# Moving banks, waits and copies in a four-stage transformer kernel: down projection, even and odd attention

## The chip, the core and the metric

The kernel runs on one core of a Trainium2 chip. A core has a matrix engine (TensorE, PE in the rows; its weight loads are PEld), a vector engine (VectorE, DVE), a scalar engine (ScalarE, ACT), GpSimd (POOL) and SyncE (SP), which issues transfers. Each follows its own list of instructions in order, and they wait for each other on semaphores. TensorE writes its results into eight PSUM banks of 128 x 512 f32. The metric is the device time of one execution in microseconds; lower is better.

## The reference, cut to what matters

512 tokens of width 1024 pass through two blocks. All tensors are f32.

```python
# first block: attention and convolution (left out here), then the FFN
x = x + conv_ffn(rms_norm(x, norm2_g), ffn_w_up, ffn_dw_w, ffn_dw_b, ffn_w_down)
#   conv_ffn: u = causal_dwconv(h @ w_up, dw_w) + dw_b;  a, v = split(u)
#             return (silu(a) * v) @ w_down              # 2816 -> 1024
x = rms_norm(x, final_g)
# second block, layer 0 ("even"): 8 dense heads (A) and 8 latent heads (B), 512 keys each
sc = q @ k.T * scale;  p = softmax(sc);  o = p @ v       # per block of 128 queries
x = x + gate * (concat(oa, ob) @ w_out)
# layer 1 ("odd"): 16 heads, |query - key| <= 128, alibi bias and a sink
sc = q @ k.T * scale - slope * |rel|                     # 3 neighbouring blocks of keys
m = max(max(sc), sink);  p = exp(sc - m)
o = (p / (sum(p) + exp(sink - m))) @ v
x = x + gate * ((o * silu(g)) @ odd_w_out)
return rms_norm(x, final_norm)
```

## The kernel before, in words

Activations are kept transposed: a chunk is 128 features by 512 tokens. Weights come in 171 units of 128 x 1024 f32. SP loads a unit into one of five slots once the unit five places before it is done (`unit_done`), and GpSimd splits it into a high and a low part (`whi`, `wlo`, lines 1040 to 1044; `w_split`). A product of a unit with the activations is made of threes of matmuls, high x high, high x low and low x high, since one alone would lose precision. Helper `unit` (line 446) makes such a product in one bank, eight threes, 24 matmuls, all recorded at line 461.

Every list of instructions is written out by hand. A bank is handed out by `bank.take(pe, pool, key)` (line 156): a pool is a tuple of bank numbers that is used in turn, with a counter that belongs to the tuple's value, and taking a bank makes TensorE wait for whoever frees its last content.

**Down stage.** The FFN's second product has 22 units (`FC`), each with all eight output chunks, so it accumulates in all eight banks at once: `down_block(i, n)` (line 754) is the three matmuls (line 760) of unit i into bank n. Unit i needs its weights and chunk i of the FFN's hidden values, `("fa", i)`. Units 0 to 17 are done one after the other, with the chunks in the order 2, 3, 6, 7, 4, 5, 1, 0; the last four (`LATE` on) chunk by chunk, so that chunk 0 is ready first and VectorE can add it to the residual (line 2085). Banks 4 and 5 hold, during the up stage before it, a copy of a vector from which VectorE makes the modulation (`ada_unit`, line 2010, `modp`); the other six are the up stage's own and are freed one by one by the depthwise convolution's last operations (lines 2026 to 2044).

**Even attention.** 32 steps (`ab_steps`), four query blocks for each of 8 pairs of heads. In step i TensorE makes the scores of step i (banks 1 and 2; line 844 or 849), the transposes of step i-2 (banks 4 and 5; line 857) and the values of step i-3 (line 870 on), with a rowsum spread every fourth step and parts of weight units as filler in the first ten. VectorE takes the scores' maximum (line 2188), ScalarE then makes the exponentials of step i (`ab_exp`, line 1445) and copies the transposed block of step i-2 out of banks 4 and 5 (`ab_copy`, line 1453), in this order.

**Even output projection.** Eight units `("eout", i)`. The first three use banks 0, 1 and 2 and are begun between the last attention steps; their last threes stand together at line 937. The other five take the pool `WIDE`, (0, 1, 2, 3). VectorE adds each result to the residual (`residual`, line 2254), which frees its bank. Behind them come the first odd units: `raw_units` takes banks 0, 1, 2 in turn, and bank 3 for the small bias products (line 478).

**Odd attention.** 32 steps again (`c_steps`), four query blocks qt for each of 8 pairs. A step has scores against two or three key blocks (256 or 384 columns; line 959), three to eight threes of an `("og", p + 1)` unit as filler (none in every fourth step, none in the last four), the transposes of step i-2 (line 969), the values of step i-3 (`c_values`, line 987), and every fourth step a spread (line 999). The values of a pair are sums over the four key blocks kt, all in the one bank 6; key block 0 was added in the second step of the pair, 1 in the third, 2 and 3 in the fourth. Bank 6 is freed by VectorE's `c_out` of the pair before (lines 2317 and 2324), which stands behind the gate of line 2164 and ahead of the next maximum (line 2290). ScalarE has exponentials (line 1518) and then the copy of one half (line 1527); VectorE copies the other half (line 2302).

## Time and profile before

| | us |
|---|---|
| median of 3 runs (1366.27 to 1368.05) | 1367.89 |
| the profiled execution | 1367.87 |
| its span, from the first instruction to the last | 1365.3 |
| TensorE busy in it | 1316.9 |
| VectorE busy | 820.5 |
| GpSimd busy | 637.6 |
| ScalarE busy | 440.2 |
| mean granted TensorE clock | 0.987 |

The profiled execution is as long as the median; 2.6 us of it lie outside the span. TensorE is busy for 96% of the span, so what it waits for, and the stretches in which its clock is low, are read one by one: the views used are the page, the waits of TensorE, the timeline and the windows.

### The profile page before, as it was taken

The page shows a single profiled execution, that of the slowest core. Times are in us where ns is not written, and L with a number is a line of the kernel's source. Part 1 is how long each engine was busy: PE and PEld are TensorE (multiplying, and loading weights), DVE is VectorE, ACT ScalarE, POOL GpSimd, SP SyncE. Part 2 cuts the span into 40 slices and gives each one's busy share as a digit, 9 for nine tenths or more (in the row PEclk, how much of TensorE's full clock was granted, in tenths as well). Part 3 has the DMA queues.
Part 4 walks back from the last instruction along what each step waited for, and adds up shares of the span by engine and source line. Part 5 has one row for each costly group of instructions (what it writes and reads, how often), then busy time and mean ns, then how long its engine had stood idle before and what let it go on. Part 6 is the DMA issues. An engine that isn't in the chain of part 4 may idle for free. (4 is left out here: it accounts for less than half of the span.)

```text
span 1365.3 us, 19690 instructions
## 1 busy us (share of the span) xinstructions
PE 1316.9 (96%) x7254; PEld 1036.5 (76%) x7254; DVE 820.5 (60%) x1586; ACT 440.2 (32%) x948; POOL 637.6 (47%) x523
## 2 busy tenths in 40 slices
PE   7999999999999999999999999999999999999996
PEld 5897766688888888888788788876556788767675
DVE  4898689914554777777572456535655254156643
ACT  4201455523122112222110332255656122244521
POOL 5865222246676666666576365532000365622230
PEclk9999999999999999999999989999999999999998
DMA  5622110112343455555543124211000123211111
GB/s 177 239 68 77 32 41 24 46 62 83 103 169 123 169 187 200 199 186 191 178 155 95 44 93 152 88 47 32 0 1 1 62 83 93 93 38 41 32 47 62
DMA packets 37522, 130.24 MB, mean 95 GB/s; under 512 B 4544, under 2 KB 4800, under 8 KB 37184
## 3 DMA queue, kind: packets, MB, share of 16 engines
q1 hardware_dynamic: 26640, 93.11, 21.3%
q10 hardware_dynamic: 10800, 35.98, 7.1%
q8 instruction: 58, 0.95, 0.3%
q14 instruction: 24, 0.20, 0.0%
HBM read 126.98 MB, written 2.10 MB: 95 GB/s over the span
## 5 line engine op out<-in xcount | busy, mean ns | idle before, releaser
L1044 POOL TENSOR_TENSOR wlo<-raw,whi 128x1024 fp32r<-128x1024 f32 x171 | 417.0, 2438 | 14.3
L1040 POOL TENSOR_TENSOR whi<-raw,ones 128x2 fp32r<-128x2 f32 x171 | 40.9, 239 | 677.5 <-DMA raw<-in_w 677.5
L461 PE MATMUL bank<-ysplit,whi 128*128 128x512 f32 x984 | 314.5, 398 | 2.1 <-DVE xbuf L2254 2.1
L461 PE MATMUL bank<-hhi,whi 128*128 128x512 f32 x536 | 218.1, 407 | 0.4 <-DVE arena L2164 0.4
L461 PEld LDWEIGHTS bank<-ysplit,whi 128*128 128x128 f32 x984 | 184.4, 190 | 38.9 <-issue 3.2
L461 PE MATMUL bank<-hhi,wlo 128*128 128x512 f32 x536 | 209.9, 392 | 0.0
L461 PE MATMUL bank<-hlo,whi 128*128 128x512 f32 x536 | 209.4, 391 | 0.0
L461 PE MATMUL bank<-ysplit,wlo 128*128 128x512 f32 x496 | 194.9, 393 | 0.0
L1041 POOL TENSOR_SCALAR whi<-raw 128x1022 fp32r<-128x1022 f32 x171 | 185.8, 1086 | 0.0
L461 PEld LDWEIGHTS bank<-hhi,whi 128*128 128x128 f32 x536 | 100.9, 188 | 25.6 <-issue 6.6
L461 PEld LDWEIGHTS bank<-hhi,wlo 128*128 128x128 f32 x536 | 100.9, 188 | 22.0
L461 PEld LDWEIGHTS bank<-hlo,whi 128*128 128x128 f32 x536 | 101.2, 189 | 18.1
L461 PEld LDWEIGHTS bank<-ysplit,wlo 128*128 128x128 f32 x496 | 94.0, 189 | 20.1
L1706 DVE SCALAR_TENSOR_TENSOR arena<-first,arena 128x512 f32<-128x512 f32 x120 | 105.6, 930 | 0.2
L1331 ACT ACTIVATE arena<-bank,cols 128x512 f32<-128x512 f32 x44 | 34.3, 779 | 177.7 <-DVE bank L2026 177.7
L760 PE MATMUL bank<-hhi,whi 128*128 128x512 f32 x176 | 70.0, 398 | 5.6 <-DVE modp L2010 3.3
L2188 DVE CUSTOM_DVE_ANT_0 arena<-bank,arena 128x512 f32<-128x512 f32 x64 | 44.2, 690 | 47.2 <-PE bank L849 28.9
L1445 ACT ACTIVATE arena<-arena,nmax,stat 128x512 f32<-128x512 f32 x64 | 51.6, 807 | 60.8 <-DVE nmax L2195 31.4
L760 PE MATMUL bank<-hlo,whi 128*128 128x512 f32 x176 | 69.7, 396 | 0.0
L760 PE MATMUL bank<-hhi,wlo 128*128 128x512 f32 x176 | 69.5, 395 | 0.0
L2026 DVE TENSOR_TENSOR bank<-bank,arena 128x512 f32<-128x512 f32 x44 | 30.7, 698 | 50.4 <-PE bank L461 50.4
L2010 DVE CUSTOM_DVE_ANT_0 arena<-bank,arena 128x512 f32<-128x512 f32 x80 | 51.7, 683 | 0.0
(315 smaller groups left out, 2100.5 us busy)
## 6 DMA issues: line engine op xcount, KB each, us to landing
raw<-in_w SPq DMA_DIRECT2D x171, 512.0 KB, 3.6
arena<-in_ada ACTq DMA_DIRECT2D x48, 512.0 KB, 4.3
xbuf<-in_xT ACTq DMA_DIRECT2D x12, 256.0 KB, 5.6
xbuf<-in_w ACTq DMA_DIRECT2D x1, 2048.0 KB, 8.9
first<-in_w ACTq DMA_DIRECT2D x1, 2048.0 KB, 8.4
out_t<-xbuf SPq DMA_DIRECT2D x8, 256.0 KB, 2.2
xbuf<-in_xT SPq DMA_DIRECT2D x4, 256.0 KB, 6.4
first<-in_uq ACTq DMA_DIRECT2D x1, 768.0 KB, 6.5
```

Source lines behind the costliest of these rows:

```text
L461: m = mm(b[:, :], w[:, s, k * P:(k + 1) * P], x, start=(k == 0 and part == 0), stop=(k == DC - 1 and part == 2))
L760: m = mm(b[:, :], w[:, u % WS, n * P:(n + 1) * P], x, start=(i == 0 and part == 0), stop=(i == FC - 1 and part == 2))
L1040: g.tensor_tensor(whi[:, s, 0:2], raw[:, s, 0:2], ones[:, :], ALU.mult)
L1041: g.tensor_scalar(whi[:, s, 2:D], raw[:, s, 2:D], 1.0, 1.0, ALU.mult, ALU.mult)\
L1044: g.tensor_tensor(wlo[:, s, :], raw[:, s, :], whi[:, s, :].bitcast(F32), ALU.subtract)\
L1331: A(ua[:, i % 4, :], bank.of(("up", i))[:, :], ACT.Identity, scale=col("ffw", order_up(i) * 3 + 2), bias=col("ffb", order_up(i)))\
L1445: A(abp[:, s % 3, half, :], abp[:, s % 3, half, :], ACT.Exp, bias=nmax[:, x:x + 1], scale=ab_scale(p, half, qt), accum_out=rsum[:, x:x + 1 ...
L1706: V.scalar_tensor_tensor(cacc[:, c, :], z[:, c, k:k + T], w, cacc[:, c, :], ALU.mult, ALU.add)\
L2010: V.tensor_tensor_reduce(ada[:, j % 2, at], bank.tiles[CACT[half]][:, :], ada[:, j % 2, at], 1.0, 0.0, ALU.mult, ALU.add, acc[:, j // (3 * ...
L2026: V.tensor_tensor(b[:, :], b[:, :], spread2, ALU.mult).then_inc(*dve_did.up(("un", i)))
L2188: link(V.tensor_tensor_reduce(abp[:, s % 3, half, :], bank.of(("S", "AB", s, half))[:, :], zero, 1.0, -3.0e38, ALU.add, ALU.max, nmax[:, x ...
```

## The change

There are five edits.

1. Down stage, start: units 0 and 1 are done together, in two parts. First chunks 2, 3 and 7 of both, then 6, 4, 5, 1 and 0 of both. The wait for `modp` stands at bank 4, no longer ahead of the stage. The later units have the order 2, 3, 7, 6, 4, 5, 1, 0.
2. Down stage, end: units 18 to 20 first add their chunks 0 and 1, each when its weights are there; then unit 21 is waited for, and its chunks 0 and 1 are added; the other chunks are as before.
3. Even output projection: units 3 to 7 take the pool (3, 0, 1, 2) in place of (0, 1, 2, 3). That tuple is the value of `E_BANKS` (line 115), too.
4. Odd attention: the values of a pair are all made in its fourth step.
5. Both attentions, ScalarE: the copy of step i-2 stands ahead of the exponentials of step i. VectorE's list is as it was.

```diff
--- before.py
+++ after.py
@@ -178,7 +178,7 @@
 H_BANKS = (6, 7)
 UP, CACT = (0, 1, 2, 3, 6, 7), (4, 5)
 N_FILL, N_S, N_O = (0,), (1, 2), (3, 6)
-EOUT_BANKS = (0, 1, 2)
+EOUT_BANKS, EOUT_REST = (0, 1, 2), (3, 0, 1, 2)
 AB_FILL_BANK, AB_S, AB_O = (0,), (1, 2), (3, 6)
 C_FILL, C_S, C_T, C_O, C_R = (0, 3), (1, 2), (4, 5), (6,), (7,)
 
@@ -762,17 +762,27 @@
                 return m
 
             LATE = FC - 4
-            pe.wait_ge(*dve_did.at(("ada", ADA_UP - 1)))
-            for i in range(FC):
-                u = UNIT[("down", i)]
-                pe.wait_ge(w_split.sem, u + 1)
+
+            def down_rows(i):
+                pe.wait_ge(w_split.sem, UNIT[("down", i)] + 1)
                 pe.wait_ge(*dve_did.at(("fa", i)))
-                for n in (2, 3, 6, 7, 4, 5, 1, 0) if i < LATE else ():
-                    if i == 0:
-                        bank.take(pe, (n,), ("down", n))
+
+            for part in (2, 3, 7), (6, 4, 5, 1, 0):
+                for i in range(2):
+                    down_rows(i)
+                    for n in part:
+                        if n == 4 and i == 0:
+                            pe.wait_ge(*dve_did.at(("ada", ADA_UP - 1)))
+                        if i == 0:
+                            bank.take(pe, (n,), ("down", n))
+                        m = down_block(i, n)
+                    if n == 0:
+                        m.then_inc(*unit_done.up(UNIT[("down", i)]))
+            for i in range(2, LATE):
+                down_rows(i)
+                for n in (2, 3, 7, 6, 4, 5, 1, 0):
                     m = down_block(i, n)
-                if i < LATE:
-                    m.then_inc(*unit_done.up(u))
+                m.then_inc(*unit_done.up(UNIT[("down", i)]))
 
             def double_sums(part):
 
@@ -784,8 +794,13 @@
                 if part:
                     m.then_inc(*pe_did.up(("fe", "sum")))
 
+            for i in range(LATE, FC - 1):
+                down_rows(i)
+                for n in range(2):
+                    down_block(i, n)
+            down_rows(FC - 1)
             for n in range(DC):
-                for i in range(LATE, FC):
+                for i in range(LATE if n >= 2 else FC - 1, FC):
                     m = down_block(i, n)
                     if n == DC - 1:
                         m.then_inc(*unit_done.up(UNIT[("down", i)]))
@@ -936,7 +951,7 @@
             for j in range(len(eout)):
                 eout[j](DC - 1)
             for i in range(len(eout), DC):
-                unit("eout", i, src=e_parts)
+                unit("eout", i, src=e_parts, pool=EOUT_REST)
             raw_units("o", 1, RAW_O, raw_o, lambda part: sums_once("o", part), lambda: spread("o", 0))
             for i in range(len(RAW_O), DC):
                 unit("oq", i, first=(lambda k: dve_did.at(("o", "h", k))) if i == len(RAW_O) else None,
@@ -971,15 +986,14 @@
                     m.then_inc(*pt_done.up(("C", i, half)))
 
             def c_values(i):
+
                 p, qt = c_steps[i]
-                if qt == 0:
+                if qt < TT - 1:
                     return
                 pe.wait_ge(*ptc.at(("C", i)))
                 pe.wait_ge(*ptd.at(("C", i)))
-                if qt == 1:
-                    bank.take(pe, C_O, ("O", "C", p))
-                b = bank.tiles[C_O[0]]
-                for kt in (qt - 1,) if qt < TT - 1 else (qt - 1, qt):
+                b = bank.take(pe, C_O, ("O", "C", p))
+                for kt in range(TT):
                     q0 = max(kt - 1, 0)
                     nq = min(kt + 1, TT - 1) - q0 + 1
                     for half in range(2):
@@ -987,8 +1001,7 @@
                         m = mm(b[64 * half:64 * half + 64, q0 * P:(q0 + nq) * P], ov[:, kt, g * HD:(g + 1) * HD],
                                pt_c(p, half, kt, q0 - kt + 1, nq), start=(kt == 0), stop=(kt == TT - 1),
                                skip_group_check=True)
-                if qt == TT - 1:
-                    m.then_inc(*pv_done.up(("C", p)))
+                m.then_inc(*pv_done.up(("C", p)))
 
             def c_spread(p):
                 pe.wait_ge(*dve_did.at(("C", "rinv", p)))
@@ -1464,10 +1477,10 @@
                 if i in PREP_V:
                     tt = i - PREP_V[0]
                     prep_copy("vB", tt, vB[:, tt, :], P)
+                if 2 <= i < n + 2:
+                    ab_copy(i - 2)
                 if i < n:
                     ab_exp(i)
-                if 2 <= i < n + 2:
-                    ab_copy(i - 2)
                 if i in PREP_K:
                     h = PREP_K[i]
                     prep_copy("KF", h, KF[h % 4][0:64, :], 64)
@@ -1531,10 +1544,10 @@
             n = len(c_steps)
             og_evac(0)
             for i in range(n + 5):
+                if 2 <= i < n + 2:
+                    c_copy(i - 2)
                 if i < n:
                     c_exp(i)
-                if 2 <= i < n + 2:
-                    c_copy(i - 2)
                 if i >= 4 and i % TT == 0 and i <= n:
                     p = i // TT - 1
                     act.wait_ge(*dve_did.at(("C", "sink", p)))
```

How TensorE's list changes is shown at three places. The first is the start of the down stage (line 760). Before, the twelve first matmuls:

```order
L760 MATMUL bank2<-hhi,whi 128x512 [waits dve_did,w_split]
L760 MATMUL bank2<-hlo,whi 128x512
L760 MATMUL bank2<-hhi,wlo 128x512
L760 MATMUL bank3<-hhi,whi 128x512 [waits dve_did]
L760 MATMUL bank3<-hlo,whi 128x512
L760 MATMUL bank3<-hhi,wlo 128x512
L760 MATMUL bank6<-hhi,whi 128x512 [waits dve_did]
L760 MATMUL bank6<-hlo,whi 128x512
L760 MATMUL bank6<-hhi,wlo 128x512
L760 MATMUL bank7<-hhi,whi 128x512 [waits dve_did]
L760 MATMUL bank7<-hlo,whi 128x512
L760 MATMUL bank7<-hhi,wlo 128x512
```

In the changed kernel, the first of each three where a bank or a wait is new:

```order
L760 MATMUL bank2<-hhi,whi 128x512 [waits dve_did,w_split]
L760 MATMUL bank2<-hlo,whi 128x512
L760 MATMUL bank2<-hhi,wlo 128x512
L760 MATMUL bank3<-hhi,whi 128x512 [waits dve_did]
...
L760 MATMUL bank7<-hhi,whi 128x512 [waits dve_did]
...
L760 MATMUL bank2<-hhi,whi 128x512 [waits dve_did,w_split]
...
L760 MATMUL bank6<-hhi,whi 128x512 [waits dve_did,w_split]
...
L760 MATMUL bank4<-hhi,whi 128x512 [waits act_did,dve_did]
```

Bank 6 is moved behind bank 7 and behind a second round over banks 2, 3 and 7, and bank 4 is the first to name what line 2010 writes. Before, a wait for that stood ahead of the first row.

The second place is the even output projection: the first matmul of each of its units 3 to 7 and, last, of the first odd unit (line 461) and its bias product (line 478). Before:

```order
L461 MATMUL bank2<-ysplit,whi 128x512 [waits dve_did,w_split]
...
L461 MATMUL bank3<-ysplit,whi 128x512 [waits dve_did,w_split]
...
L461 MATMUL bank0<-ysplit,whi 128x512 [waits dve_did,w_split]
...
L461 MATMUL bank1<-ysplit,whi 128x512 [waits dve_did,w_split]
...
L461 MATMUL bank2<-ysplit,whi 128x512 [waits dve_did,w_split]
...
L461 MATMUL bank0<-ysplit,whi 128x512 [waits dve_did,w_split]
...
L478 MATMUL bank3<-shr,whi 128x2 [waits dve_did]
```

In the changed kernel:

```order
L461 MATMUL bank0<-ysplit,whi 128x512 [waits dve_did,w_split]
...
L461 MATMUL bank1<-ysplit,whi 128x512 [waits dve_did,w_split]
...
L461 MATMUL bank2<-ysplit,whi 128x512 [waits dve_did,w_split]
...
L461 MATMUL bank3<-ysplit,whi 128x512 [waits dve_did,w_split]
...
L461 MATMUL bank0<-ysplit,whi 128x512 [waits dve_did,w_split]
...
L461 MATMUL bank0<-ysplit,whi 128x512 [waits dve_did,w_split]
...
L478 MATMUL bank3<-shr,whi 128x2 [waits dve_did]
```

Unit 3 has bank 0 in place of bank 2; unit 7 had bank 2 and now has bank 0, which the first odd unit takes next.

The third place is the odd attention, within one pair: transposes, values and scores in the third step, and values and scores in the fourth. Before (lines 969, 987, 959):

```order
L969 MATMUL bank4<-ident,arena 128x128 [waits ptc,p_ready]
L969 MATMUL bank4<-ident,arena 128x128
L969 MATMUL bank5<-ident,arena 128x128 [waits ptd,p_ready]
L969 MATMUL bank5<-ident,arena 128x128
L987 MATMUL bank6<-arena 64x384 [waits ptd,ptc]
L987 MATMUL bank6<-arena 64x384
L959 MATMUL bank1<-split_r,ysplit 128x384 [waits sm_ready]
...
L987 MATMUL bank6<-arena 64x384 [waits ptd,ptc]
L987 MATMUL bank6<-arena 64x384
L987 MATMUL bank6<-arena 64x256 x2
L959 MATMUL bank1<-split_r,ysplit 128x256 [waits sm_ready]
```

In the changed kernel the same three lines are 984, 1001 and 974:

```order
L984 MATMUL bank4<-ident,arena 128x128 [waits ptc,p_ready]
L984 MATMUL bank4<-ident,arena 128x128
L984 MATMUL bank5<-ident,arena 128x128 [waits ptd,p_ready]
L984 MATMUL bank5<-ident,arena 128x128
L974 MATMUL bank1<-split_r,ysplit 128x384 [waits sm_ready]
...
L984 MATMUL bank4<-ident,arena 128x128 [waits ptc,p_ready]
L984 MATMUL bank4<-ident,arena 128x128
L1001 MATMUL bank6<-arena 64x256 [waits dve_did,ptd,ptc]
L1001 MATMUL bank6<-arena 64x256
L1001 MATMUL bank6<-arena 64x384 x4
L1001 MATMUL bank6<-arena 64x256 x2
L974 MATMUL bank1<-split_r,ysplit 128x256 [waits sm_ready]
```

The third step has no values now, and the fourth has those of all four key blocks, with the wait for bank 6 (`dve_did`).

## Rows read from the trace of the kernel before

**Rows 1.** Page: busy us and share by engine, and TensorE clock by fortieth
```profile
PE 1316.9 (96%) x7254; PEld 1036.5 (76%) x7254; DVE 820.5 (60%) x1586; ACT 440.2 (32%) x948; POOL 637.6 (47%) x523
...
PEclk9999999999999999999999989999999999999998
```

**Rows 2.** Waits of TensorE, whole span: engine, place <- releaser: us, times, longest
```profile
PE bank L857 <- ACT arena L1453: 5.5, 7, 2.2
...
PE bank L760 <- DVE modp L2010: 3.3, 1, 3.3
...
PE bank L987 <- DVE arena L2324: 2.1, 2, 1.6
```

**Rows 3.** Timeline at the start of the down stage: start, us, engine, line, operation
```profile
660.03 0.69 DVE L2010 CUSTOM_DVE_ANT_0 arena<-bank,arena 128x512 f32<-128x512 f32 x1
...
660.77 0.79 PE L760 MATMUL bank<-hhi,whi 128*128 128x512 f32 x1 [3.33 <-DVE modp L2010]
...
662.81 0.69 DVE L2044 TENSOR_TENSOR arena<-bank,arena 128x512 f32<-128x512 f32 x1
...
664.10 0.40 PE L760 MATMUL bank<-hhi,wlo 128*128 128x512 f32 x1
...
675.67 0.39 PE L760 MATMUL bank<-hhi,wlo 128*128 128x512 f32 x1
```

**Rows 4.** Timeline at the last four units of the down stage, TensorE
```profile
762.64 0.66 PE L760 MATMUL bank<-hhi,whi 128*128 128x512 f32 x1 [2.26 <-POOL wlo L1044]
...
766.36 0.39 PE L760 MATMUL bank<-hhi,whi 128*128 128x512 f32 x1
```

**Rows 5.** Timeline of the even output projection and of what follows it
```profile
1076.29 1.44 DVE L2254 SCALAR_TENSOR_TENSOR xbuf<-bank,modc,xbuf 128x512 f32<-128x512 f32 x2 [8.38 <-PE bank L461]
...
1078.84 0.74 DVE L2254 SCALAR_TENSOR_TENSOR xbuf<-bank,modc,xbuf 128x512 f32<-128x512 f32 x1
...
1079.73 0.79 PE L461 MATMUL bank<-ysplit,whi 128*128 128x512 f32 x2 [2.10 <-DVE xbuf L2254]
...
1109.03 0.40 PE L461 MATMUL bank<-ysplit,whi 128*128 128x512 f32 x1
...
1109.23 0.75 DVE L2254 SCALAR_TENSOR_TENSOR xbuf<-bank,modc,xbuf 128x512 f32<-128x512 f32 x1 [2.50 <-PE bank L461]
```

**Rows 6.** Windows: a stretch; busy us of each engine; TensorE clock; DMA
```profile
1080.20:1083.70 3.50, 3.50 (x10) 2.68 (x10) 0.64 (x2) 0.66 (x2) 3.42 (x3) 0.51 0.51 199
```

**Rows 7.** Timeline at the end of the even attention
```profile
1050.25 1.04 PE L857 MATMUL bank<-ident,arena 128*128 128x128 f32 x8
...
1052.18 0.81 ACT L1445 ACTIVATE arena<-arena,nmax,stat 128x512 f32<-128x512 f32 x1 [2.54 <-DVE nmax L2195]
...
1053.79 1.05 ACT L1453 ACTIVATE arena<-bank 128x512 f32<-128x512 f32 x2
...
1054.51 1.11 PE L857 MATMUL bank<-ident,arena 128*128 128x128 f32 x8 [2.20 <-ACT arena L1453]
```

**Rows 8.** Timeline of the odd attention, an inner step and the end
```profile
1233.98 0.48 DVE L2290 CUSTOM_DVE_ANT_0 arena<-bank,arena 128x256 f32<-128x256 f32 x1
...
1234.27 0.65 PE L987 MATMUL bank<-arena 128*64 128x256 f32 x4
...
1234.85 0.79 PE L959 MATMUL bank<-split_r,ysplit 64*128 64x384 f32 x6
...
1292.38 0.65 PE L987 MATMUL bank<-arena 128*64 128x256 f32 x4 [1.59 <-DVE arena L2324]
...
1292.56 0.48 DVE L2290 CUSTOM_DVE_ANT_0 arena<-bank,arena 128x256 f32<-128x256 f32 x1
...
1293.19 0.80 PE L959 MATMUL bank<-split_r,ysplit 64*128 64x384 f32 x6 [0.15 <-DVE nmax L2290]
...
1303.56 1.97 PE L987 MATMUL bank<-arena 128*64 128x384 f32 x12
...
1305.33 1.07 PE L999 MATMUL bank<-ident,rinv 128*64 128x128 f32 x16
```

## The prediction

> **What bounds the kernel now.** I read the page first: TensorE is busy for 1316.9 of 1365.3 us [rows 1], so the time is its list of instructions, plus its waits, plus what a low clock adds. The clock line has one tenth less in three places of forty, so low stretches are short and have to be looked for in the timeline. Then I read the waits of TensorE: 5.5 us for ScalarE's copies in the even attention, 3.3 us for `modp` ahead of the down stage, 2.1 us for bank 6 in the odd attention [rows 2]. The timeline shows two more, 2.26 us for weights before the last four down units [rows 4] and 2.10 us for a bank in the even output projection [rows 5]. The edits aim at just these five. For each I ask whether the wait goes, and what is late next.
>
> **Clock.** Three of the waits are followed by matmuls at half rate. At full rate 51 matmuls of the down stage take 675.67 - 664.10 = 11.57 us, 0.227 each; after the first wait, the 8 intervals from 660.77 to 664.10 take 3.33 us in place of 1.82, so 1.5 us are lost [rows 3]. After the second, the 9 intervals from 762.64 to 766.36 take 3.72 us in place of 2.04, 1.7 lost [rows 4]. After the third the granted clock is 0.51, 1.2 GHz, for 3.5 us [rows 6], again 1.7 us lost. The 2.20 us wait at 1054.51 and the 1.59 us one at 1292.38 are followed by transposes and values in which I see no such stretch [rows 7, 8]. A wait that goes takes its low stretch with it.
>
> **Start of the down stage.** The first matmul can start at the end of the up stage, 3.33 us before 660.77 [rows 3], so near 657.4, if banks 2, 3 and 7 are free; they belonged to convolutions finished earlier, since those of the last two up units hold banks 0 and 1. Part one is 18 matmuls, 4.1 us, until 661.5. Bank 6 is the first of part two; bank 4, three matmuls on, is wanted at 662.2, when the last read of it, at 660.03 for 0.69 us, is done [rows 3]. Bank 0 is last, behind another 9 matmuls, at about 664.2; VectorE's last operation on it starts at 662.81 and takes 0.69 us, until 663.5 [rows 3]. All waits are covered, the tightest by 0.7 us. Gain 3.3 + 1.5 = 4.8 us. The slots of units 0 and 1 come free later within their pair, but unit 1 is done after 48 matmuls, 10.9 us, as ever.
>
> **Last four units.** TensorE waits 2.26 us for unit 21 [rows 4]. Units 18 to 20 now bring 3 x 2 x 3 = 18 matmuls, 4.1 us, ahead of it: the wait is covered with 1.8 us to spare. Chunk 0 is finished 21 matmuls after the start in place of 12, 2.0 us later, but chunk 1 after 24 as before, and VectorE's first step with chunk 0 is one addition alone. Gain 2.3 + 1.7 = 4.0 us.
>
> **Copies first, even attention.** At the end, the transposes at 1050.25 could be copied 0.72 us later (1053.79 to 1054.51 is what lies between a copy's start and the transposes that it frees a bank for, and I take the same the other way), at 1051.0. But exponentials that begin at 1052.18 stand ahead, so the copy starts at 1053.79 and TensorE waits 2.20 us [rows 7]. Copies first, it finds its bank at about 1051.7. Exponentials begin no sooner than the maximum allows, 1052.18, by which time a copy of 1.05 us from 1051.0 is done [rows 7]: nothing is delayed. All seven waits, 5.5 us [rows 2], have this form. TensorE then reaches the next scores sooner and could wait for VectorE's maximum; I take that at 0, at worst half is given back. Gain 5.5 us, bounds 2.7 and 5.5.
>
> **Even output projection.** Unit 3 now takes bank 0, which VectorE frees with the first of the two operations of 1.44 us from 1076.29, at 1077.0 [rows 5]. TensorE wants it 2.10 us before 1079.73, at 1077.6. The wait goes, and the low stretch: 2.1 + 1.7 = 3.8 us. But the counter of the tuple (3, 0, 1, 2) has run on through nine E units and stands at its second entry, so unit 7 gets bank 0 again, and the first odd unit, which takes bank 0, waits for the addition of unit 7. That addition starts at 1109.23; it takes 0.75 us, and from the end of such an addition to TensorE's start is 0.15 (1078.84 + 0.74 to 1079.73) [rows 5]. The unit starts at 1110.1 in place of 1109.03: a new wait of 1.1 us. Net gain 2.7 us (1.0 if this wait too were followed by a low stretch).
>
> **Values in the fourth step, odd attention.** The number of matmuls is the same. A short block of values has a start of its own: 4 records of 256 columns from 1234.27 to 1234.85 take 0.58 us, 12 with four times the columns from 1303.56 to 1305.33 take 1.77, 0.44 for a quarter [rows 8]; 0.14 us for each of 16 blocks that go is 2.2 us at most. But where bank 6 was waited for, VectorE is what is late: it has the gate, `c_out` and then the maxima in a row, and TensorE's next scores need the second of these. From the second maximum at 1292.56 to the scores at 1293.19 is 0.63 us. So these scores stay at 1293.19, whether or not values stand ahead of them: the 1.59 us wait for bank 6 [rows 8] becomes one of 2.4 us for the maxima. Within the pairs the same rule caps the gain: the second maximum at 1233.98 allows scores at 1234.6, 0.24 us sooner than 1234.85 [rows 8], and not the 0.58 of the block. The other 0.34 us are lost again in the fourth step, and what remains of merging is about 0.05 a pair, 0.4 in all. At the end the last pair loses: its 12-record block could begin beside the last copies, now all 16 records, 1.77 x 1.25 = 2.2 us, wait for them. I put 0.44 us for the extra quarter and 0.66 for the copy (0.55 us and its signals, an estimate by the lengths above), 1.1 us. Net: a loss of 0.7 us; bounds from a gain of 2.1 + 2.2 = 4.3 to a loss of 2.5 (0.7 and a low stretch of 1.7 after the new wait of 2.4). ScalarE's order in this stage changes little: TensorE waited for its copies only in the last steps.
>
> **Sum.** 4.8 + 4.0 + 5.5 + 2.7 - 0.7 = 16.3 us. The profiled execution took 1367.87 us, within 0.02 of the median, so the time follows as 1367.87 - 16.3 = 1351.6 us.
>
> **A rule on the clock.** All three waits that I credit with a low stretch have one in the trace [rows 3, 4, 6], and others do not [rows 7, 8]. The Trainium skill, "TensorE: Matmul & The Clock Gate", section "What's actually happening", says that the activity monitor runs freely and does not start with the kernel, so that where the clock turns differs from run to run. By that rule only a part of the 4.9 us is there in the average execution; by the rows it is all there. Its result is rival 1.
>
> **Rivals.**
> 1. The low stretches are chance: the median before holds about half of them, and as many appear elsewhere after. For it: waits of 2.26 and 2.10 us had one, one of 2.20 had none. Against: the profiled run has all three and is no slower than the median. Gain 16.3 - 2.4 = 13.9, or, with one more after the 2.4 us wait, 12: 1354 to 1356 us.
> 2. Values in one block pay: VectorE is not what is late, both waits for bank 6 go and the block starts are saved. Against it stand the maxima at 1292.56. 16.3 + 0.7 + 4.3 = 21.3: 1346.6 us.
> 3. Copies first only move the wait in the even attention to the scores' banks. Gain 16.3 - 2.7: 1354.3 us.
> 4. The other side: the fourth step, 1 us longer by its values, pushes the scores that follow it, so VectorE enters each pair's chain of gate, `c_out` and maxima late and the 2.4 us wait that I expect once appears in all eight pairs, 19 us. It decides if the fourth step's delay exceeds what filler covers. 1367.9 - 17.0 + 19.2 = 1370.1 us. Against: seven of the pairs have eight threes of filler, and only there does VectorE have 0.2 us and more to spare.
> 5. A bank that is not free in the down stage makes edit 1 do nothing: 16.3 - 4.8 gives 1356.4 us.
>
> **Numbers.** My forecast 0.55, rival 1 0.17, rival 2 0.08, rival 3 0.12, rival 4 0.03, rival 5 0.05. The range is 1347.5 to 1356: it holds the forecast, rivals 1 and 3, and part of 2, and the bounds of the even attention and of the new wait. What a measurement can tell from no change is 0.2%, 2.7 us. Faster by more 0.95, within 0.02, slower 0.03.
>
> **What would show it.** Right: no wait of TensorE for `modp`, for GpSimd at the last four down units, or for the residual at unit 3; a new wait of about 1.1 us at the first odd unit; waits for the copies of the even attention near 0; in the odd attention a single wait of about 2.4 us for the maxima in the first step without filler, and the stage from first scores to first output matmul as long as before, within 1 us. Wrong: a wait for bank 6 that remains, waits of the even scores for the maxima, or low stretches where TensorE had no wait.

## The result and the profile after

| | before | changed |
|---|---|---|
| median of 6 runs of each, us | 1367.97 | 1357.82 |
| ratio of the changed kernel to before | | 0.992 [0.990, 0.994] |
| profiled execution, us | 1367.87 | 1353.58 |
| its span, us | 1365.3 | 1351.7 |
| mean granted TensorE clock | 0.987 | 0.988 |

The kernel became faster by 10.2 us. The forecast was 16.3 us and a range that ends at 1356.0, so direction and most of the mechanism were right and the time was not. (Three executions, two of before at 2616.91 and 1881.66 us and one of a later kernel at 7383.49 us, were disturbed and are left out of every ratio and mean below.)

The page of the changed kernel, its busy row of TensorE and its clock row; they answer to [rows 1].

```profile
PE 1310.5 (97%) x7254; PEld 1036.2 (77%) x7254; DVE 831.6 (62%) x1586; ACT 442.6 (33%) x948; POOL 646.0 (48%) x523
...
PEclk9999999999999999999999989999999999999898
```

The number of matmuls is the same, 7254. TensorE is busy 6.4 us less with them. But the clock row has a new 8, third from the end. The waits of TensorE behind it (engine, place, releaser: us, times, longest):

```profile
PE bank L974 <- DVE nmax L2303: 4.0, 8, 2.3
PE bank L974 <- DVE arena L2177: 3.5, 1, 3.5
...
PE bank L461 <- POOL wlo L1057: 0.9, 1, 0.9
```

Of the waits of [rows 2], those for the copies of the even attention, for `modp` and for bank 6 are all gone. In their place stand three that before did not have: 2.3 us for a maximum, 3.5 us for line 2177 at the scores of the odd attention, and 0.9 us in a unit. (Lines of the changed kernel are 13 to 15 higher from the down stage on: scores 974, transposes 984, values 1001, spread 1012, gate 2177, residual 2267, maximum 2303.)

**The down stage** answers to [rows 3, 4]. All matmuls of line 760 as a group (count, shortest/median/longest ns, first and last start):

```profile
L760 PE MATMUL bank<-hhi,whi x176: 389/389/389, 655.0 to 774.0; 128*128 128x512 f32 x176
L760 PE MATMUL bank<-hlo,whi x176: 389/389/389, 655.3 to 774.3; 128*128 128x512 f32 x176
L760 PE MATMUL bank<-hhi,wlo x176: 389/389/389, 655.5 to 774.5; 128*128 128x512 f32 x176
its engine sat idle before it (us, times) until:
who waited for it (us, times):
```

Nothing stands under "sat idle", so not one of the 528 matmuls waits, and the longest is as short as the median, so none ran at the low clock. The first stands at 655.04, and the `modp` that held it before is ready only 3.4 us later:

```profile
655.04 0.39 PE L760 MATMUL bank<-hhi,whi 128*128 128x512 f32 x1
...
658.39 0.08 DVE L2023 DVE_READ_ACCUMULATOR2_ANT modp<- 128x1 f32 x1
```

**The even attention** answers to [rows 7]. Near its end the copies now run ahead of the exponentials, and the transposes after them have no wait:

```profile
1030.39 1.08 ACT L1466 ACTIVATE arena<-bank 128x512 f32<-128x512 f32 x2 [0.88 <-PE bank L872]
1031.62 0.81 ACT L1458 ACTIVATE arena<-arena,nmax,stat 128x512 f32<-128x512 f32 x1
...
1034.38 1.04 PE L872 MATMUL bank<-ident,arena 128*128 128x128 f32 x8
```

**The even output projection** answers to [rows 5]. The 2.10 us wait is gone, and the new one that the prediction named is there, behind the addition of unit 7:

```profile
1087.20 0.75 DVE L2267 SCALAR_TENSOR_TENSOR xbuf<-bank,modc,xbuf 128x512 f32<-128x512 f32 x1 [2.57 <-PE bank L461]
...
1088.05 0.47 PE L461 MATMUL bank<-ysplit,whi 128*128 128x512 f32 x1 [0.89 <-POOL wlo L1057]
```

The row names GpSimd, whose instruction ended at 1088.02 by the profile. VectorE's addition ended at 1087.95. Which of the two the matmul waited for can't be told from this row; an experiment below tells it.

**Start of the odd attention.** This is the place that the prediction did not look at:

```profile
1168.83 0.60 PE L504 MATMUL bank<-ident,arena 128*128 128x128 f32 x4
...
1170.08 1.28 ACT L1523 ACT_TABLE_LOAD   x1
1171.37 0.60 ACT L1523 ACTIVATE arena<-bank 128x512 f32<-128x512 f32 x1
1172.10 0.69 DVE L2177 SCALAR_TENSOR_TENSOR arena<-arena,bank 128x512 f32<-128x512 f32 x1 [19.10 <-ACT arena L1523]
...
1172.93 0.62 PE L974 MATMUL bank<-split_r,ysplit 64*128 64x256 f32 x6 [3.51 <-DVE arena L2177]
...
1176.05 0.63 PE L461 MATMUL bank<-hhi,whi 128*128 128x512 f32 x1
...
1176.48 0.63 PE L461 MATMUL bank<-hlo,whi 128*128 128x512 f32 x1
```

The gate of the first pair (`("og", 0)`, lines 1523 and 2177) reads its unit out of a bank, and the first odd scores want that bank. So they wait for a table load of ScalarE (1.28 us), its activation and VectorE's multiplication. Then the filler runs 0.43 us apart (1176.05 to 1176.48) in place of 0.227: the low clock.

**End of the odd attention** answers to [rows 8]. VectorE has `c_out`, then the two maxima, and the scores start 0.15 us behind the second:

```profile
1274.39 0.69 DVE L2337 TENSOR_TENSOR arena<-bank,arena 128x512 f32<-128x512 f32 x1
1275.00 0.47 DVE L2303 CUSTOM_DVE_ANT_0 arena<-bank,arena 128x256 f32<-128x256 f32 x1
...
1275.40 0.48 DVE L2303 CUSTOM_DVE_ANT_0 arena<-bank,arena 128x256 f32<-128x256 f32 x1
...
1276.03 1.32 PE L974 MATMUL bank<-split_r,ysplit 64*128 64x384 f32 x6 [2.34 <-DVE nmax L2303]
```

This is the single wait of "about 2.4 us for the maxima" of the prediction. It is the only long one: the other seven of its row above are 0.2 to 0.3 us, five of them one to a pair, which is the time that the prediction has "lost again in the fourth step". From the first odd scores to the first output matmul the stage now takes 120.0 us (1172.93 to 1292.96) in place of 115.9 (1190.48 to 1306.34). The prediction named "as long as before, within 1 us" as a sign of being right, and this one is missed.

Windows behind the two large new waits, and behind each the next stretch (us, busy and count of TensorE, its weight loads, VectorE, ScalarE, GpSimd; clock; DMA):

```profile
1173.50:1176.50 3.00, 3.00 (x10) 2.32 (x9) 0.90 (x4) 1.09 (x4) 2.92 (x2) 0.53 0.00 0
1176.90:1180.00 3.10, 3.10 (x17) 2.09 (x15) 1.17 (x4) 1.19 (x4) 0.00 (x0) 0.97 0.00 0
1276.10:1279.10 3.00, 2.70 (x12) 1.89 (x14) 1.94 (x8) 2.22 (x9) 0.00 (x0) 0.50 0.00 0
1279.10:1282.40 3.30, 3.30 (x16) 1.90 (x16) 2.15 (x7) 2.05 (x7) 0.00 (x0) 0.50 0.00 0
1282.70:1287.00 4.30, 4.30 (x44) 2.81 (x41) 1.81 (x7) 1.47 (x5) 0.00 (x0) 0.98 0.00 0
```

At 0.50 the clock is 1.2 GHz. In all, 3.4 us of it follow the wait for the gate (1173.7 to 1177.1) and 6.8 us the wait for the maxima (1276.1 to 1282.9), 1.7 and 3.4 us lost.

**Where the time came from,** by the shift between the two traces (start before minus start after of the same instruction; growth is gain): 9.1 us in the down stage, 7.5 in the even attention, 2.0 in the even output projection and the odd projections. Then it shrinks, from 20.3 us at the last matmuls ahead of the odd attention (1189.15 before, 1168.83 after) to 17.5 at its first scores (1190.48, 1172.93), 16.7 at its first transposes (1199.27, 1182.53) and 13.9 at its last scores (1298.18, 1284.23).

**One measure for all that follows.** The same kernel varies from run to run by more than most edits are worth (before: 1363.2 to 1377.4 us over 46 runs). Each run has a span and a mean granted clock. Span times clock is what the span would be at 2.4 GHz throughout, "at full clock" below. The rest of the span is the clock's share. (Low clock while TensorE idles counts in it too, so only differences of the share mean something. And the clock is recorded to 0.001, which leaves up to 0.7 us of error in a single run.) For before, the first has a standard deviation of 0.9 us and the second one of 2.7: nearly all the scatter is the clock's. The table has all undisturbed runs of each kernel that have a span and a clock on record; behind ± is the standard error of the mean.

| kernel | runs | median us | at full clock | clock's share |
|---|---|---|---|---|
| before | 46 | 1368.0 | 1346.7 ± 0.1 | 19.0 ± 0.4 |
| changed | 12 | 1358.3 | 1335.9 ± 0.2 | 19.1 ± 1.0 |
| changed, gate's unit in bank 3 | 6 | 1354.7 | 1334.2 ± 0.2 | 17.4 ± 1.0 |
| and the last even unit in bank 2 ("both mended") | 10 | 1349.6 | 1332.7 ± 0.4 | 14.7 ± 1.2 |
| and the odd values as before | 10 | 1347.5 | 1332.0 ± 0.2 | 13.2 ± 0.8 |
| both mended, odd copies late | 4 | 1352.1 | 1333.9 ± 0.3 | 15.9 ± 0.7 |
| before, gate's unit in bank 2 | 7 | 1372.2 | 1348.5 ± 0.3 | 22.1 ± 1.1 |
| before, values block alone | 12 | 1370.2 | 1347.4 ± 0.2 | 19.8 ± 1.0 |
| before, down stage alone | 6 | 1356.6 | 1340.2 ± 0.3 | 14.4 ± 1.2 |
| before, even copies alone | 6 | 1361.5 | 1340.5 ± 0.2 | 18.3 ± 0.9 |
| before, output projection's pool alone | 12 | 1371.2 | 1347.3 ± 0.1 | 21.9 ± 1.0 |

### The profile page after: what moved, and what is told of

Read it like the earlier page. It is cut to its first block and busy times, and to the rows that moved or that the text cites. A ratio compares the mean times of both kernels' runs of the same rounds, so it can differ in the third digit from the quotient of the medians.

```text
span 1351.7 us, 19676 instructions
## 1 busy us (share of the span) xinstructions
PE 1310.5 (97%) x7254; PEld 1036.2 (77%) x7254; DVE 831.6 (62%) x1586; ACT 442.6 (33%) x948; POOL 646.0 (48%) x523
## 5 line engine op out<-in xcount | busy, mean ns | idle before, releaser
L1053 POOL TENSOR_TENSOR whi<-raw,ones 128x2 fp32r<-128x2 f32 x171 | 46.0, 269 | 655.8 <-DMA raw<-in_w 655.7
L461 PEld LDWEIGHTS bank<-hlo,whi 128*128 128x128 f32 x536 | 101.2, 189 | 18.3
L461 PEld LDWEIGHTS bank<-ysplit,wlo 128*128 128x128 f32 x496 | 93.7, 189 | 19.8
```

The source lines that it names most:

```text
L461: m = mm(b[:, :], w[:, s, k * P:(k + 1) * P], x, start=(k == 0 and part == 0), stop=(k == DC - 1 and part == 2))
L1053: g.tensor_tensor(whi[:, s, 0:2], raw[:, s, 0:2], ones[:, :], ALU.mult)
```

## The experiments

### The changed kernel again

No edit.

> The changed kernel once more, nothing edited, as the reference for the kernels beside it and to see another profiled execution. Bank theory: the waits of TensorE are the same (3.5 us ahead of the first odd scores, 2.3 us ahead of the scores of step 29 of the odd attention, 1.1 us at the first odd unit), but the low stretches of the clock are not in the same places, and the times spread over 5 us or more about 1357.8. Rival, the profiled execution is the rule and the slower ones are disturbed: time 1353 to 1355, the same low stretches.

Measured: 1358.25 us, ratio 0.991 [0.989, 0.994]. The waits are those of the first trace, 3.5 us for the gate and 2.3 for the maxima among them. The result stands, and the shortfall against the forecast is no accident of one series.

### The gate's unit back in bank 3

```diff
-            unit("og", 0)
+            unit("og", 0, pool=(3,))
```

> The changed kernel with the unit og 0 put into bank 3, as before the change, in place of bank 2. Bank theory: the wait of 3.5 us ahead of the first odd scores becomes the 0.7 us of before, the wait of 0.34 us ahead of og 0 goes, and so does the low stretch behind it (1.0 us in the profiled execution): 4.2 us less than the changed kernel, near 1353.6 by its median. Rival, the first scores wait for ScalarE's table load in any case: 0 to 0.5 us less.

Measured: 1354.74 us, ratio 0.989 [0.987, 0.991]; at full clock 1.7 us less than the changed kernel (of the 2.8 us between the waits of 3.5 and 0.7, the next maximum takes 0.7 back). The timeline at the first odd scores:

```profile
1176.69 1.28 ACT L1523 ACT_TABLE_LOAD   x1
...
1176.77 0.62 PE L974 MATMUL bank<-split_r,ysplit 64*128 64x256 f32 x6 [0.73 <-issue]
...
1178.72 0.69 DVE L2177 SCALAR_TENSOR_TENSOR arena<-arena,bank 128x512 f32<-128x512 f32 x1 [18.54 <-ACT arena L1523]
```

The scores now start while ScalarE loads its table, 2 us ahead of the gate's multiplication. So the 3.5 us wait was for a bank. The code says why that bank had changed. The five units of the even output projection used to advance the counter of `WIDE`, (0, 1, 2, 3). With a pool of their own they don't, five takes are missing, and `("og", 0)`, which is taken from `WIDE`, gets bank 2 in place of 3. Bank 2 is one of the two banks of the odd scores.

### And a pool whose last unit takes bank 2

```diff
-EOUT_BANKS, EOUT_REST = (0, 1, 2), (3, 0, 1, 2)
+EOUT_BANKS, EOUT_REST = (0, 1, 2), (3, 0, 1, 0, 2)
```

> As the one with og 0 in bank 3, and units 3 to 7 of the even output projection in banks 3, 0, 1, 0, 2 in place of 0, 1, 2, 3, 0, so that the first odd unit's bank 0 was freed long before. Bank theory: the 1.1 us wait at the first odd unit goes, 1.1 us less than with og 0 alone, near 1352.5. Rival, the trace names GpSimd's split (line 1057) for that wait, and if weights are what is late, nothing is gained by the banks.

Measured: 1348.47 us, ratio 0.986 [0.984, 0.988]. The 0.9 us wait is gone from the trace though GpSimd's list is as before, so it had been for the bank and not for `wlo`. At full clock the gain is 0.9 ± 0.5 us in the same series and 1.5 ± 0.4 over all runs. The clock's share fell as well, by 2.7 ± 1.6 over all runs.

### Before, with the gate's unit in bank 2

```diff
-            unit("og", 0)
+            unit("og", 0, pool=(2,))
```

> The kernel before with only the unit og 0 moved from bank 3 to bank 2, the price of that bank by itself. Bank theory: a wait of 3.5 us ahead of the first odd scores in place of 0.7, and mostly a low stretch behind it: 3 to 5 us slower than before, 1371 to 1373. Rival: no change, 1368.

Measured: 1372.2 us, ratio 1.004 [1.002, 1.006]. At full clock +1.9 ± 0.3 us, clock's share +3.1 ± 1.2. The one bank costs, in the kernel before, what its mending gives in the changed one, and the trace has the wait for line 2164 with the same 3.5 us.

### Both mended, with the odd values as before

The edit puts the old `c_values` back.

> The kernel with both banks mended (1348.5 us), with the odd values as before: head by head, in the fifth and sixth step. Theory A, values in the fourth step cost time: the waits of TensorE in the odd attention add up to 6.0 us with the block (2.34 before the 29th head's scores, 0.76, 0.34, 0.57, 0.57, and 1.4 at the first scores) and to 3.6 without it, and the 2.34 us wait has a 1.2 GHz stretch behind it that costs 1.7, so 2.4 + 1.7 = 4.1 us less: 1344.4 us, and no wait over 1.6 us in the odd attention. Theory B, the block is worth the 0.7 us of the prediction and the lost time is the clock's doing whatever waits there are: 1349.2 us. A time within 1 us of 1348.5 favours B.

> Both banks mended and the odd values as before, again. Theory A, the block of values costs its 2.34 us wait and the low stretch behind it: at full clock 1.5 us less than with the block (1331.8), and 3 us less as measured, 1345.5. Theory B, the block costs only the prediction's 0.7 us: 1347.8 as measured, as the first comparison had it.

> The kernel with both banks mended again, beside the next one on the same chip. 1333.3 us at full clock and 1348.5 as measured the first time; the same within 1 and 2 us is expected under each theory.

Theory B in the first of these texts has the sign wrong: the prediction's 0.7 us was a loss, as the second has it. Nor does the old code go "head by head": it adds key block by key block, in three steps of a pair. Measured: 1347.78 us the first time, on another chip than its partner. The second time, beside it on the same chip, 1347.16 us, ratio 0.985 [0.983, 0.987], against 1350.36 us, 0.987 [0.985, 0.989]; every run without the block is faster than every run with it (1344.60 to 1348.86 against 1349.39 to 1351.63). At full clock over all runs the block costs 0.7 ± 0.4 us and of the clock's share 1.5 ± 1.4. But the two comparisons don't agree on how it divides: on the same chip the block costs nothing at full clock (-0.5 ± 0.5) and 4.5 ± 0.9 of the clock's share, against 1.6 ± 0.5 and -0.8 ± 2.3 the first time. So theory A's total of 3 us is met on the one chip, and its 1.5 us at full clock is not shown. The waits of the odd attention without the block are 1.5 and 0.9 us for bank 6, and no scores wait over 0.7 us. The rows without the block:

```profile
PE bank L1002 <- DVE arena L2339: 2.4, 2, 1.5
...
PE bank L974 <- DVE nmax L2305: 1.1, 3, 0.7
```

With it the maxima have 5.2 us in 9 waits. All waits of the stage together are 7.4 us with the block and 4.3 without. The 3.1 us between them, less the 2.2 that the prediction allows at most for 16 block starts, leave 0.9, near the 0.7 at full clock.

### Before, with the values block alone

The edit is the fourth of the change, on the kernel before.

> The kernel before (1368.0 us) with the block of values of a pair in the fourth step alone; all banks as before. Theory A, the block costs 2.4 us of waits and 1.7 us of the clock behind the 2.34 us wait: 1372.1 us. Theory B, the prediction's -0.7 us: 1367.3 us. Theory C, with late copies the waits that the block brings are in part covered by others: 1368 to 1370 us.

Theory B has the wrong sign here too; right is 1368.7 us. Measured: 1370.19 us, ratio 1.001 [0.999, 1.003]; at full clock +0.8 ± 0.2 us. The wait for the maxima is in its trace with 2.39 us. Theory A's 2.4 us at full clock is out; between B and C the time, with a standard error of 1.0, doesn't decide. So the block is a small loss at full clock, as predicted, and the ratio alone could not tell it from nothing.

### Both mended, with ScalarE's copies late in the odd attention

```diff
-                if 2 <= i < n + 2:
-                    c_copy(i - 2)
                 if i < n:
                     c_exp(i)
+                if 2 <= i < n + 2:
+                    c_copy(i - 2)
```

> The kernel with both banks mended (1348.5 us), with the copies of ScalarE behind the exponentials again in the odd attention alone. Theory A, as predicted, in the odd attention the order of copy and exponential carries nothing: 1348 to 1349 us, and the 2.34 us wait before the 29th head's scores stays. Theory B, copies ahead of exponentials push the exponentials and with them the maxima, and make the 2.34 us wait: it goes, with its 1.7 us of low clock, 1344.5 us. Theory C, late copies bring waits of the spread and of the values' turn for ScalarE, about 0.5 us a pair late in the stage: 1350 us or more.

Measured: 1352.12 us, ratio 0.988 [0.985, 0.992]. The 2.4 us wait for the maxima stays, so B falls. The trace has three waits of TensorE for this copy, 0.31 to 0.36 us, in place of one of 0.34, but all waits of the stage together grow by only 0.3. At full clock it costs 1.2 ± 0.5 us against both mended. That is on the side of C, and its interval overlaps that of both mended (0.986 [0.984, 0.988]): copies first in the odd attention may be worth up to a microsecond.

### Before, with the down stage alone

The edits 1 and 2 of the change, on the kernel before.

> The kernel before (1368.0 us) with the new order of the down stage alone. Theory A: the shift between the two traces grew by 9.1 us in this stage, 4.8 + 4.0 were predicted with the 1.2 GHz stretches behind the two waits (1.5 and 1.7), and taking the waits away takes these stretches away: 1359.0 us. Theory B, the low stretches come by chance and the waits alone are worth 3.3 + 2.3 = 5.6: 1362.4 us. The new order doesn't change the counters of banks that the odd attention uses, or it does: then the first odd scores wait 3.5 us here too and the gain is 4 to 5 us smaller.

Measured: 1356.60 us, ratio 0.992 [0.989, 0.995], 11.4 us under the median of all runs of before. At full clock 6.5 ± 0.3 us, against 5.6 for the two waits alone. Of the clock's share 4.6 ± 1.3, against 1.5 + 1.7. Both sizes exceed theory A a little; theory B, waits without clock, is out. The first odd scores wait 0.7 us as before, so the new order moves no counter that they need. This edit alone gives as much as all five together.

### Before, with the even copies alone

```diff
+                if 2 <= i < n + 2:
+                    ab_copy(i - 2)
                 if i < n:
                     ab_exp(i)
-                if 2 <= i < n + 2:
-                    ab_copy(i - 2)
```

> The kernel before with copies ahead of exponentials in the even attention alone. Times are compared as they are and as span times mean granted clock (the kernel before: 1346.7 us over 29 runs, standard deviation 0.8), which takes the number of low clock stretches of the single execution out. Theory A, the prediction's 5.5 us for the waits of TensorE alone: 1341.2 us at full clock, about 1363 as measured. Theory B, the ledger's 7.5 us between the two traces: 1339.2 at full clock, 1361 as measured; then something other than the listed waits goes too. Theory C, the wait moves to the banks of the scores: 1344 at full clock and waits for line 2188 above 2 us.

Measured: 1361.47 us, ratio 0.995 [0.993, 0.997]; at full clock 6.2 ± 0.2 us, of the clock's share 0.7 ± 0.9. Between A and B at full clock. All seven waits for the copies are gone. The scores wait no more than before: the row has the same 0.5 us, so C falls.

```profile
PE bank L844 <- DVE nmax L2188: 0.5, 1, 0.5
```

### Before, with the output projection's pool alone

```diff
-EOUT_BANKS = (0, 1, 2)
+EOUT_BANKS, EOUT_REST = (0, 1, 2), (3, 0, 1, 2)
...
-                unit("eout", i, src=e_parts)
+                unit("eout", i, src=e_parts, pool=EOUT_REST)
```

> The kernel before with the pool (3, 0, 1, 2) for the units 3 to 7 of the even output projection alone. Theory A, the counter of the old pool explains the missing time: five takes fewer put the gate's unit into bank 2, so the first odd scores wait 3.5 us in place of 0.7, and the first odd unit waits 0.9 us for bank 0; at full clock 1346.7 - 2.1 + 0.9 + 1.8 = 1347.3 us, no faster than before, the low stretch behind the 2.1 us wait gone and one behind the 3.5 us wait in its place: 1368.6 as measured. Theory B, the prediction's account of this edit: a gain of 2.7, 1365.2 us, and the first odd scores wait 0.7 us.

Measured: 1371.19 us, ratio 1.002 [1.001, 1.004]; at full clock 1347.3, as theory A has it to a tenth. Its time of 1368.6 is 2.6 us short, since it exchanges one low stretch for one other. The edit that was to give 2.7 us costs 0.6 ± 0.2 at full clock, and of the clock's share another 2.9 ± 1.1. In the profiled execution 6.9 us of low clock follow the 3.5 us wait, and behind the old 2.1 us wait it was 3.4. Its waits, and the window behind the 3.5 us one:

```profile
PE bank L959 <- DVE arena L2164: 3.5, 1, 3.5
PE bank L461 <- POOL wlo L1044: 0.9, 1, 0.9
```

```profile
1193.40:1199.80 6.40, 5.58 (x19) 4.06 (x21) 1.57 (x5) 1.09 (x4) 3.58 (x3) 0.50 0.00 0
1200.40:1205.00 4.60, 4.60 (x23) 3.37 (x24) 2.33 (x8) 2.23 (x7) 0.00 (x0) 1.00 0.01 4
```

### The fastest version

Both banks mended and the odd values as before: 1347.5 us over ten runs, 1.5% under before and 0.8% under the changed kernel. Its page (the execution with a span of 1344.4 us):

```profile
PE 1308.9 (97%) x7254; PEld 1032.9 (77%) x7254; DVE 834.1 (62%) x1586; ACT 442.8 (33%) x948; POOL 643.7 (48%) x523
...
PEclk9999999999999999999999989999999999999998
```

The new 8 of the changed kernel's clock row is gone.

## Why the prediction was wrong, step by step

- **Start of the down stage, 3.3 + 1.5, and last four units, 2.3 + 1.7: right, somewhat small.** 5.6 predicted at full clock, 6.5 measured; 3.2 of the clock, 4.6 ± 1.3 measured. No bank was late (rival 5 falls).
- **Copies first, 5.5 us: right, 0.7 too small.** 6.2 at full clock. The forecast stood at the upper bound of its own bracket, 2.7 to 5.5, and the truth lay above it. Rival 3 falls.
- **Even output projection, +2.7 us: this step failed.** The prediction followed one counter, that of the tuple that the edit now uses, and so found the wait at the first odd unit (1.1 us predicted, 0.9 measured). It did not follow the counter of the pool that the edit stops using. That one also hands out the bank of the gate's unit, at the end of all the odd projections, some 80 us later. Alone, this edit gave -0.6 us at full clock in place of the +1.0 (2.1 - 1.1) that the prediction counts without the clock, and it raised the clock's share by 2.9 where 1.7 less was expected. By the means of the times it cost 3.4 us in place of giving 2.7, 6.1 us off, more than the 5.2 by which the whole forecast missed; the down stage (10.9 for 8.8) and the even copies (6.9 for 5.5) gave more than predicted, and the values alone cost 1.8 for 0.7.
- **Values in the fourth step, -0.7 us: right at full clock as far as is known** (0.8 ± 0.2 on the kernel before; 0.7 ± 0.4 on the mended one, where its two series disagree), with the wait of 2.3 us where it was named. Its low stretch was in the bounds ("0.7 and a low stretch of 1.7") and not in the sum. It belonged in the sum.
- **The clock, 4.9 us: this term failed in sum, not in kind.** The sentence was "A wait that goes takes its low stretch with it". It held: the clock's share fell by 5.8 ± 0.9 us in the fastest version, which has none of the three waits with a credited stretch and none of the new ones (its waits for bank 6 are as before). But the same rule was not applied to waits that come. In the changed kernel the share is 19.1 ± 1.0 against 19.0 ± 0.4: the waits for the gate (3.1 ± 1.2 of the share, alone on the kernel before) and for the maxima (1.5 ± 1.4) brought back about what the three others had given.

The account by the means of all runs: 16.3 predicted, of it 11.4 at full clock (5.6 + 5.5 + 1.0 - 0.7) and 4.9 of the clock. Measured 10.7 at full clock, 0.0 ± 1.1 of the clock, and 0.4 outside the span (2.1 against 2.5), together 11.1; the medians of the first series say 10.2. What is missing is the clock's term almost alone. At full clock the error of 1.6 in the output projection was made up by the 0.9 and 0.7 that the down stage and the even copies gave more.

**What the rows of before already showed.** The prediction says that the clock row has one tenth less in three places of forty. [rows 1] has it in two: the 24th, 785 to 819 us, and the last. Neither is one of the three stretches that the sum credits. The 24th is a stretch of 10.2 us behind the down stage where TensorE had no wait (the last section has it), the last is the end of the kernel. So "low stretches where TensorE had no wait", which the prediction lists as a sign of being wrong, stood in the trace from which it was made, and again in that of the changed kernel.

**The rivals.** Rival 5 has the nearest time, 1356.4 us, by a reason that did not occur, and rival 1 the next (its 12 us "with one more after the 2.4 us wait") by a reason that is half right. Counted over the 14 profiled executions of all kernels, a low stretch stood right behind the 3.3 and 2.2 us waits of the down stage in 5 of 5 each, behind the 2.1 us wait of the output projection in 5 of 5, behind the wait for the maxima in 7 of 7 and for the gate in 4 of 4. It stood behind the 2.2 us wait of the even attention in 2 of 5, behind a wait of 2.0 to 2.2 us in the attention of the first block (line 568, no edit touches it) in 4 of 14, behind the 1.6 us wait for bank 6 in 3 of 7, behind the 0.9 us wait in none of 4. So the waits that the sum credits, and the two large new ones, have theirs every time, and chance or the work around them decides at the others (length alone does not: waits of 2.1 and 2.2 us have it always in two places, in 2 of 5 and 4 of 14 in two others). The length varies too: 3.4 us behind each wait that the sum credits, but 3.4 or 6.8 behind the two new ones. The Trainium skill, "TensorE: Matmul & The Clock Gate", section "What's actually happening", has the activity monitor run freely, so that where the clock turns differs from run to run. The rows agree with it in the two attentions and at bank 6. At the waits of the sum the stretch came every time, so the prediction was right to count it in full. Rivals 2 to 5 fall: the block of values doesn't pay (2), the waits of the even attention did not move (3), the long wait for the maxima appears once and not in all eight pairs (4), no bank was late in the down stage (5).

**What stays open.** That the clock's share fell by 2.7 ± 1.6 us with the 0.9 us wait, though no low stretch stood behind that wait in any trace, isn't explained; with this error it may be nothing. The one profiled execution with that wait had 13.7 us of low clock in the first 600 us, the two without it none and 6.8 us, and no edit touches that part, so chance is the nearer reading. Nor is it known why the down stage and the even copies give 0.9 and 0.7 us more at full clock than their waits.

## What to carry to other kernels

When an edit takes some takers out of a shared pool that is used in turn, list every later taker of the old pool as well as of the new one: the cost may come up at an instruction that the diff doesn't touch. In a stream that keeps TensorE full, price every wait of 2 us or more, the new ones as the old ones, at its length and another 1.7 to 3.4 us for the low clock behind it; five of the seven such places counted here had that in every execution, and two in attention stages only now and then. And where runs scatter more than the edits are worth, compare the span times the mean granted clock: here it brought the standard deviation from 2.5 down to 0.9 us and showed effects of 0.7 us that the ratios of the times could not tell from nothing.

## What the runs showed of the hardware that was not expected

A low stretch without any wait. Just behind the down stage, where the norm's sums begin, 10.2 us at 1.2 GHz stand in 11 of the 14 profiled executions, a shorter one in one, and none in two. In the kernel before:

```profile
793.50:803.70 10.20, 10.20 (x37) 9.04 (x37) 1.55 (x9) 0.18 (x1) 9.61 (x9) 0.50 0.16 51
```

The same work, in windows of the changed kernel and of before with the values block alone:

```profile
781.00:791.00 10.00, 10.00 (x38) 8.85 (x37) 1.54 (x9) 0.18 (x1) 9.75 (x10) 0.51 0.04 7
```

```profile
790.00:800.00 10.00, 9.82 (x67) 8.65 (x66) 1.55 (x9) 0.84 (x2) 9.75 (x10) 1.00 0.35 123
```

TensorE is full in both, with 38 records of matmuls in the first and 67 in the second. The stretch costs about 5 us where it stands. Shortly before it TensorE had 16 matmuls of a single column (line 532, 1.84 us in the changed kernel); the two executions without the stretch have them as well. Whether they help to bring the clock down was not tried.

An execution without it is not always a fast one. The one above, at 1364.70 us, is 5.5 us under the median of its kernel, but the other, before with the gate's unit in bank 2, at 1373.81 us is 1.6 over its own, with 13.7 us of low clock in its first 600 us. That part, which no edit touches, varies more: it holds between 0 and 17.1 us of low clock in the 14 executions, up to 8.5 us of time. The largest, in the mended kernel with the odd values as before, the first time:

```profile
139.50:146.40 6.90, 6.90 (x27) 5.14 (x25) 3.36 (x10) 1.78 (x7) 3.57 (x3) 0.51 0.00 0
265.80:269.20 3.40, 3.40 (x22) 2.62 (x22) 3.40 (x9) 1.31 (x4) 0.00 (x0) 0.50 0.02 5
293.10:300.00 6.90, 6.90 (x20) 5.55 (x21) 0.16 (x1) 0.00 (x0) 3.58 (x3) 0.51 0.02 7
```

So two executions can differ by this much with nothing changed, and a single profiled execution doesn't tell what an edit did to the clock.
